# Attention scores of one transformer layer in five fp32r passes instead of two fp32 matmuls

## What is computed

```
q = (rms_norm(cq, q_norm_g) @ w_uq)      # 8 heads of 128 + 64 columns
kv = (rms_norm(ckv, kv_norm_g) @ w_ukv)  # 8 heads of 128 (keys) + 128 (values)
q_lat = concat([q_nope, axial_rope(q_rope)])
k = concat([k_nope, broadcast(axial_rope(k_rope))])   # 256 latent + 256 context tokens
s = einsum('bqhd,bkhd->bhqk', q, k) * 192 ** -0.5
out = softmax(s) @ v
```

## Time and profile before

| | us |
|---|---|
| median of three runs | 2856.29 (2855.32 to 2858.62) |
| profiled execution, its own time | 2855.02 |
| span of the profiled execution | 2853.2 |
| PE busy | 2775.5 (97% of the span) |
| DVE busy | 1699.8 (60%) |
| ACT busy | 901.1 (32%) |
| first score starts, last score starts (from the span's start) | 1941.79, 2024.4 |

### The profile page before, as it was taken

One profiled execution on the slowest core, in us unless ns is written; L12 is line 12 of the kernel. 1 busy time (PEld: TensorE's weight loads), 2 busy tenths in 40 slices (PEclk: granted clock), 3 DMA queues, 4 the chain that ended last, 5 costly groups with the idle time before them and its releaser, 6 DMA issues.

```text
span 2853.2 us, 33123 instructions
## 1 busy us (share of the span) xinstructions
PE 2775.5 (97%) x12983; PEld 2293.5 (80%) x12983; DVE 1699.8 (60%) x1740; ACT 901.1 (32%) x830; POOL 7.0 (0%) x15
## 2 busy tenths in 40 slices
PE   6999999999999999999999899999989999999998
PEld 4778888888888888878877788887878888888886
DVE  6866756666575756565645843465564555555556
ACT  6631212122121212112112522354353333333333
POOL 0000000000000000000000000000000000000000
PEclk9999999999999999999999999999999999999999
DMA  9956555555554657676755442432355555555553
GB/s 312 303 193 191 170 150 158 163 160 162 147 176 132 196 158 255 191 245 188 232 170 176 111 118 89 131 106 80 118 171 173 187 186 190 191 191 190 182 188 132
DMA packets 408016, 496.83 MB, mean 174 GB/s; under 512 B 19090, under 2 KB 277512, under 8 KB 407176
## 3 DMA queue, kind: packets, MB, share of 16 engines
q1 hardware_dynamic: 407196, 493.10, 55.3%
q0 software_dynamic: 496, 2.63, 0.3%
q10 hardware_dynamic: 252, 0.10, 0.0%
HBM read 493.69 MB, written 2.10 MB: 174 GB/s over the span
## 4 chain that ended last, share of the span: by engine, by line
PE 83%; DVE 4%; ACT 3%; issue 2%; DMA 2%; SPq 0%; DVEq 0%; ACTq 0%
PE py L944 8%; PE py L946 8%; PE py L945 8%; PE pg L944 5%; PE pg L946 5%; PE pg L945 5%; PE pu L946 5%; PE pu L945 5%; PE pu L944 5%; ACT wh L562 2%; PE py L1378 2%; PE py L1380 2%; PE py L1379 2%; PE pg L1359 1%; PE pg L1360 1%
## 5 line engine op out<-in xcount | busy, mean ns | idle before, releaser
L1450 DVE TENSOR_TENSOR wl<-raw,wh 128x2048 fp32r<-128x2048 f32 x342 | 783.7, 2291 | 832.5 <-ACT wh L562 832.3
L562 ACT ACTIVATE wh<-raw 128x2048 fp32r<-128x2048 f32 x342 | 654.1, 1914 | 1361.8 <-PE py L946 495.8
L944 PE MATMUL py<-ah,wh 128*128 128x512 f32 x704 | 276.8, 393 | 6.2 <-DVE xy L1612 5.1
L946 PE MATMUL py<-ah,wl 128*128 128x512 f32 x704 | 274.8, 390 | 0.0
L945 PE MATMUL py<-al,wh 128*128 128x512 f32 x704 | 274.6, 390 | 0.0
L944 PE MATMUL pu<-hh,wh 128*128 128x512 f32 x656 | 255.8, 390 | 0.0
L944 PE MATMUL pg<-hh,wh 128*128 128x512 f32 x656 | 255.5, 389 | 0.0
L946 PE MATMUL pu<-hh,wl 128*128 128x512 f32 x656 | 255.2, 389 | 0.0
L946 PE MATMUL pg<-hh,wl 128*128 128x512 f32 x656 | 255.2, 389 | 0.0
L945 PE MATMUL pu<-hl,wh 128*128 128x512 f32 x656 | 255.2, 389 | 0.0
L945 PE MATMUL pg<-hl,wh 128*128 128x512 f32 x656 | 255.2, 389 | 0.0
(11 more groups left out here) (420 smaller groups left out, 4605.2 us busy)
## 6 DMA issues: line engine op xcount, KB each, us to landing
raw<-in_ffn_w_in SPq DMA_DIRECT2D x170, 1024.0 KB
chunk<-in_ada_w SPq DMA_DIRECT2D x189, 512.0 KB, 3.9
raw<-in_ffn_w_out SPq DMA_DIRECT2D x88, 1024.0 KB
raw<-in_ada_w SPq DMA_DIRECT2D x64, 512.0 KB
raw<-in_mix_w_in SPq DMA_DIRECT2D x30, 1024.0 KB
accc<-in_ada_w SPq DMA_DIRECT2D x35, 512.0 KB, 4.7
raw<-in_mix_w_out SPq DMA_DIRECT2D x16, 1024.0 KB
war<-in_ffn_w_in SPq DMA_DIRECT2D x16, 384.0 KB, 5.1
```

The costliest lines, as they stand in the source:

```text
L562: nc.scalar.activation(wh[:, slot % 2, :], raw[:, slot, :], ACT.Copy).then_inc(wh_ready, 1)
L944: mm(out_ap, w[0], xh_ap, start=first, stop=False, skip_group_check=True)
L946: return mm(out_ap, w[1], xh_ap, start=False, stop=last, skip_group_check=True)
L1450: tt(wl[:, slot % 2, :], raw[:, slot, :], wh[:, slot % 2, :].bitcast(F32), ALU.subtract).then_inc(wl_ready, 1)
```

## The change

The scores are made in five fp32r passes of 512 columns each. For that, the copies `qn` and `kn` are written by ACT as fp32r (the high parts) and DVE subtracts them from the PSUM bank to get the low parts `qnl` and `knl`; it counts `upl_ready`, and PE may reuse a bank only when the low part is out too. The shared rotary key becomes `krh` (high, ACT) and `krl` (low, DVE). For the rotary queries, a tile `qs` of 128 partitions holds for each head the 64 high rows in one half and the 64 low rows in the other, so that one pass over 128 partitions against `krh` (which holds the rotary key twice) covers high x high and low x high; one pass over 64 partitions against `krl` covers high x low. `qs` is made two heads at a time by `rope_high` (two ACT copies of 64 x 256) and `rope_low` (two DVE subtractions of 64 x 256): the first pair before the attention stage, the three others inside its steps a = 0, 2 and 4. The turning of the retention output moves on PE from before the values slab to behind its sixth bank, with a wait for all four rotations, since `qs` takes the place of `yret`. ACT's `y_high` and DVE's `y_low` move with it, and so do the splits of the slab after. No load is added or moved on SP's or POOL's queue.

```diff
@@ -180,9 +180,12 @@
     cql = at("cql", [P, QT, LAT], F32R, o_e + 4 * KB)
     ckvh = at("ckvh", [P, CT, TOK], F32R, o_hl + 20 * KB)
     ckvl = at("ckvl", [P, CT, TOK], F32R, o_hl + 24 * KB)
-    qn = at("qn", [P, HEADS, LAT], F32, o_hl + 8 * KB)
+    qn = at("qn", [P, HEADS, LAT], F32R, o_hl + 8 * KB)
+    qs = at("qs", [P, HEADS, LAT], F32R, o_hh + 24 * KB)
     qr = at("qr", [P, HEADS // 2, LAT], F32, o_a)
-    kn = at("kn", [P, HEADS, TOK], F32, o_xc)
+    kn = at("kn", [P, HEADS, TOK], F32R, o_xc)
+    knl = [at("knl0", [P, 4, TOK], F32R, o_hh + 8 * KB), at("knl1", [P, 4, TOK], F32R, o_e)]
+    krl = at("krl", [P, TOK], F32R, o_e + 12 * KB)
     vm = [at("vm0", [P, 4, 4 * P], F32, o_a + 8 * KB), at("vm1", [P, 4, 4 * P], F32, o_hl)]
     pt = [at("pt0", [P, 4, LAT], F32, o_hl + 16 * KB), at("pt1", [P, 4, LAT], F32, o_e + 8 * KB)]
     pn = at("pn", [P, 2, TOK], F32, o_hl + 28 * KB)
@@ -203,6 +206,8 @@
     ropes = at("ropes", [P, 4, LAT], F32, o_m + 4 * P * 4)
     sgn = at("sgn", [P, 2, 512], F32, o_m + 4 * P * 4)
     act = sm("act", [P, TOK])
+    qnl = [at("qnl0", [P, 4, LAT], F32R, o_a + 4 * KB), at("qnl1", [P, 2, LAT], F32R, o_e + 14 * KB),
+           at("qnl2", [P, 2, LAT], F32R, small[0])]
     rms = sm("rms", [P, TOK])
     rope_t = sm("rope_t", [P, LAT])
     vt = sm("vt", [P, VROWS])
@@ -217,6 +222,7 @@
     csp = sm("csp", [P, 4 * KT + P], F32R)
     rstd = sm("rstd", [P, 12])
     ssum = at("ssum", [P, TOK], F32, small[0])
+    krh = at("krh", [P, TOK], F32R, small[0])
     rows = sm("rows", [4, 2 * BLK])
     hf = at("hf", [P, 2, TOK], F32, o_m + 4 * P * 4)
     dec = sm("dec", [P, 2 * HEADS])
@@ -291,7 +297,8 @@
     rs_done, rp_ready, ry_done, ry_free = sem("rs_done"), sem("rp_ready"), sem("ry_done"), sem("ry_free")
     yst_ready, ysd_ready, yn_ready, y_turned = sem("yst_ready"), sem("ysd_ready"), sem("yn_ready"), sem("y_turned")
     mixh_ready, mixl_ready, rg_ready, rgs_ready = sem("mixh_ready"), sem("mixl_ready"), sem("rg_ready"), sem("rgs_ready")
-    up_done, up_free = sem("up_done"), sem("up_free")
+    up_done, up_free, upl_ready = sem("up_done"), sem("up_free"), sem("upl_ready")
+    krh_ready, qsh_ready, qs_ready = sem("krh_ready"), sem("qsh_ready"), sem("qs_ready")
     sc_done, nm_ready, exp_done, pn_ready = sem("sc_done"), sem("nm_ready"), sem("exp_done"), sem("pn_ready")
     turned, pt_ready, o_done, oh_ready, ol_ready = sem("turned"), sem("pt_ready"), sem("o_done"), sem("oh_ready"), sem("ol_ready")
     sgn_ready, gu_ready, act_turned = sem("sgn_ready"), sem("gu_ready"), sem("act_turned")
@@ -312,6 +319,9 @@
     XBANKS = py + pgu
     EARLY_BANKS = ((2, pg, pu), (0, py[0], py[1]), (1, py[2], py[3]))
+
+    def qn_low(h):
+        return qnl[0][:, h, :] if h < 4 else qnl[h // 2 - 1][:, h % 2, :]
     def pair(bank_ap):
         return bank_ap.rearrange("p (a n) -> p a n", a=2)
@@ -779,6 +789,8 @@
             static_split(MIX0 + S_UQ + 1)
             se.wait_ge(decay_ready, HEADS)
             nc.scalar.activation(ckvh[:], ckv[:], ACT.Copy).then_inc(cqh_ready, 1)
+            se.wait_ge(rope_done, 9)
+            nc.scalar.activation(krh[:], krope[:], ACT.Copy).then_inc(krh_ready, 1)
             gates_out(1)
             values_out(1)
             def gates_silu():
@@ -816,11 +828,20 @@
             static_split(MIX0 + S_UQ + 4)
             for h in range(HEADS):
                 up(12 + h, kn[:, h, :], py[h % 4][:])
+            def rope_high(j):
+                se.wait_ge(rope_done, 9 + j + 1)
+                for lo in (0, ROPE):
+                    ins = nc.scalar.activation(qs[lo:lo + ROPE, 2 * j + lo // ROPE, :], qr[lo:lo + ROPE, j, :], ACT.Copy)
+                ins.then_inc(qsh_ready, 1)
+
+            se.wait_ge(yn_ready, 1)
             for k in range(4):
-                y_high(k)
-            static_split(MIX0 + S_UQ + 5)
-            se.wait_ge(mixl_ready, 4)
-            for k in range(4):
+                if k == 3:
+                    se.wait_ge(y_turned, 4)
+                    rope_high(0)
+                    for j in range(4):
+                        y_high(j)
+                    static_split(MIX0 + S_UQ + 5)
                 for half in range(2):
                     j = 20 + 2 * k + half
                     up(j, vm[half][:, k, :], py[j % 4][:])
@@ -853,6 +874,8 @@
                 probs(a)
                 if a + 2 < 16:
                     exps(a + 2)
+                if a in (0, 2, 4):
+                    rope_high(a // 2 + 1)
                 if a % 2 == 1:
                     static_split(MIX0 + S_OUTR + a // 2 + 1)
             out_high(HEADS - 1)
@@ -1228,7 +1251,11 @@
             def up_bank(k):
-                if k >= 4:
+                if 4 <= k < 12:
+                    pe.wait_ge(upl_ready, k - 3)
+                elif 16 <= k < 24:
+                    pe.wait_ge(upl_ready, k - 7)
+                elif k >= 12:
                     pe.wait_ge(up_free, k - 3)
                 return py[k % 4]
@@ -1262,9 +1289,6 @@
                     ins = three(b[:], w_at(m, t * 1024 + h * P, t * 1024 + (h + 1) * P), ckvh[:, t, :], ckvl[:, t, :],
                                 t == 0, t == CT - 1)
                 ins.then_inc(up_done if h < HEADS - 1 else slab_used, 1)
-            pe.wait_ge(yn_ready, 1)
-            for k in range(4):
-                y_turn(k)
             m = MIX0 + S_UKV + 1
             pe.wait_ge(wl_ready, m + 1)
             for k in range(4):
@@ -1277,11 +1301,14 @@
                         mm(b[:], xl_ap, w_h, start=False, stop=False)
                         ins = mm(b[:], xh_ap, w_l, start=False, stop=(t == CT - 1))
                     ins.then_inc(up_done if (k, half) != (3, 1) else slab_used, 1)
-                if k == 0:
-                    pe.wait_ge(mixl_ready, 4)
                 if k < 2:
                     for j in (2 * k, 2 * k + 1):
                         swap(9 + j, qr[:, j, :], 2)
+                if k == 2:
+                    pe.wait_ge(yn_ready, 1)
+                    pe.wait_ge(rope_done, 13)
+                    for j in range(4):
+                        y_turn(j)
             def scores(a):
@@ -1290,14 +1317,22 @@
                     pe.wait_ge(exp_done, a - 2)
                 else:
                     pe.wait_ge(up_free, 25 + a)
+                if a % 4 == 0:
+                    pe.wait_ge(qs_ready, a // 4 + 1)
                 lo = (h % 2) * ROPE
                 b = py[a % 3]
-                mm(b[:], qn[:, h, k * P:(k + 1) * P], kn[:, h, :], start=True, stop=False)
-                mm(b[:], qr[lo:lo + ROPE, h // 2, k * P:(k + 1) * P], krope[lo:lo + ROPE, :], start=False, stop=True).then_inc(sc_done, 1)
+                o = slice(k * P, (k + 1) * P)
+                mm(b[:], qn[:, h, o], kn[:, h, :], start=True, stop=False)
+                mm(b[:], qn[:, h, o], knl[h // 4][:, h % 4, :], start=False, stop=False)
+                mm(b[:], qn_low(h)[:, o], kn[:, h, :], start=False, stop=False)
+                mm(b[:], qs[:, h, o], krh[:], start=False, stop=False)
+                mm(b[:], qs[lo:lo + ROPE, h, o], krl[lo:lo + ROPE, :], start=False, stop=True).then_inc(sc_done, 1)
             def turn(a):
                 pe.wait_ge(pn_ready, a + 1)
-                if a >= 2:
+                if a < 2:
+                    pe.wait_ge(mixl_ready, a + 1)
+                else:
                     pe.wait_ge(pt_ready, a - 1)
                 for j in range(4):
                     ins = nc.tensor.transpose(pgu[a % 2][:, j * P:(j + 1) * P], pn[:, a % 2, j * P:(j + 1) * P], ident)
@@ -1319,7 +1354,6 @@
                                     mixh[:, head0 + k, :], mixl[:, head0 + k, :], k == 0 and d == 0, k == HEADS - 1)
                 ins.then_inc(slab_used, 1)
-            pe.wait_ge(rope_done, 13)
             scores(0)
             scores(1)
             for a in range(16):
@@ -1333,6 +1367,7 @@
                     pe.wait_ge(wl_ready, MIX0 + S_OUTR + h + 1)
                     if h == 0:
                         pe.wait_ge(up_free, 28)
+                        pe.wait_ge(mixl_ready, 4)
                     pe.wait_ge(y_free, Y_OUT + h)
                     out_slab(MIX0 + S_OUTR + h, py[3], 0)
                     if h < HEADS - 1:
@@ -1804,12 +1839,25 @@
             ve.wait_ge(cqh_ready, 1)
             tt(cql[:], cq[:], cqh[:].bitcast(F32), ALU.subtract).then_inc(lat_split, 1)
             static_split(MIX0 + S_UQ + 1)
+
+            def up_low(k, out_ap, in_ap, high):
+                ve.wait_ge(up_free, k + 1)
+                tt(out_ap, in_ap, high.bitcast(F32), ALU.subtract).then_inc(upl_ready, 1)
+
+            def query_lows(h0, h1):
+                for h in range(h0, h1):
+                    up_low(h, qn_low(h), py[h % 4][:, 0:LAT], qn[:, h, :])
+
             ve.wait_ge(cqh_ready, 2)
             tt(ckvl[:], ckv[:], ckvh[:].bitcast(F32), ALU.subtract).then_inc(lat_split, 1)
+            ve.wait_ge(krh_ready, 1)
```

(26 more changed lines are left out.)

## The result

The changed kernel takes 2862.14 us (median of 11 runs, 2860.36 to 2865.1) against 2855.63 us of the kernel before (11 runs): ratio 1.0021, 95% interval 1.0013 to 1.0029. It is slower by 6.5 us. Forecast were 2857.6 us and no change, so the time lies above the range.

What follows compares the result with a forecast made beforehand. PE was taken to bound the kernel; -9.2 (scores) + 2.5 (before the first score) + 2.1 (fill) + 5.9 (three steps) = +1.3 us on the profiled 2855.02, forecast 2857.6 us, no change; range 2852.5 to 2860.8.

Steps and rivals of the forecast that it cites:

- the first paragraph's rule: PE bounds the values and attention stages: a pass taken out is worth its full time, a wait costs its full time.
- The fill: Filling the softmax pipeline before turn(0): row_max(0) stands behind DVE's split, so PE stands 2.1 us.
- A rotary step: Attention steps 0, 2 and 4: row_norm stands behind rope_low, PE stands about 2.0 us each, 5.9 us together.
- part 3: Three attention steps with a rotary pair: a 3.3 us chain from turn(a) to turn(a + 1) makes PE wait, 5.9 us.
- the scores: Attention stage: each of 16 scores falls from 2.10 to 1.53 us, a gain of 9.2 us.
- The stretch ahead: Before the first score: PE waits for DVE's low parts and the values slab's split, together 2.5 us.
- The wait for the fourth rotation: Before the moved transposes on PE: costs nothing, rotations end at 1938.8, PE's sixth values bank at 1939.0.
- The new score: Five fp32r passes in 1.53 us, keeping 0.4 us for going to the 64-partition form and back.
- Rival 1: Scores: tiling switches go away with short passes, 15.6 us less on PE but longer stalls, net -2 us, 2854.4; chance 0.2.
- rival 2: Lows hide: no waits in the rotary steps, fill under 1 us; 2844 to 2850.6 us, faster; chance 0.08.
- Rival 3: Slower: the switch inside fp32r costs more, at 0.43 each +8.7 us, 2865; chance 0.06 with dearer rotary operations.
- a dearer pass: Scores: the 64-partition pass runs like its fp32 forerunner, 0.43 instead of 0.23 us, +3.2 us, the range's upper end.

Runs made afterwards that it cites:

- both orders: Changed kernel with rotary pairs made in steps 1, 3, 5 and the first output slab's split moved early: 2849.91 us, ratio 0.9973 to the kernel before.
- full-pass run: Changed kernel with the fifth pass of each score over all 128 partitions instead of 64: 2857.69 us, ratio 1.0001 to the kernel before.
- filler run: Changed kernel with ten useless fp32r passes on PE between scores(2) and turn(0): 2859.98 us, ratio 1.0014 to the kernel before.

## Why the prediction was wrong

**The part that failed** is the first paragraph's rule: "a wait put in costs its full time". A wait costs that and, in most of the profiles with waits of over 2 us, a stretch at half clock from within the wait or right behind it. The working read the clock as 1.00 in both windows of the kernel before and carried it over to a kernel with four waits of 2 us and more, although none of the rows that it rested on showed such a wait. The trace did: the 2.25 us wait at 1272 us above, with 0.50 behind it. Neither the sum nor a rival had a term for it. It is 4.0 of the 6.0 us that the attention stretch came out above the forecast; without it the profiles would differ by 3.0 us, inside the forecast range (up to 4.5 above the kernel before).

**The other 2.0 us are sizes.** The waits of fill and steps are 9.66 us instead of 8.0. The fill is 2.45 (7.05 - 4.60) instead of 2.1; row_max(0) starts 7.4 us behind the turns instead of 6.7, mostly because the two rotary copies ahead of it take longer (0.85 us instead of 0.56, begun 0.3 us after the turns). A rotary step is (9.66 - 2.45) / 3 = 2.4 instead of 2.0: the 64 x 256 copies on ACT and subtractions on DVE, which no row of the kernel before showed, take 0.41 and 0.42 us each and do not overlap, so a pair is 0.83 and 0.85 us, where the working had 0.6 and 0.7. Timelines of ACT and DVE after:

```profile
1953.37 0.83 ACT L834 ACTIVATE qs<-qr 64x256 fp32r<-64x256 f32 x2
```
```profile
1954.23 0.85 DVE L1889 TENSOR_TENSOR qs<-qr,qs 64x256 fp32r<-64x256 f32 x2 [2.44 <-ACT qs L834]
1955.12 0.16 DVE L1907 RECIPROCAL rrec<-rsum 128x1 f32<-128x1 f32 x1
```

They show the chain of part 3 as it was forecast: the reciprocal of step 1 stands behind a subtraction that waits 2.44 us for ACT. And the scores are worth 8.85 instead of 9.2 us (with both orders).

**What was right.** The stretch ahead: 2.25 us for 2.5, in the places named. Laid pass by pass beside the kernel before, the changed one loses 0.3 us at query bank 5 (forecast 0.4), 0.2 at bank 8 (0.1), 0.6 at key bank 16 (0.85) and 1.2 at the values (1.1); the view of waits lists only part of this (none, 0.3, 0.3 and 0.9). The wait for the fourth rotation cost nothing. The new score: 1.54 for 1.53 us, with the change of form kept, which the full-pass run confirms. The places of the four stalls, and the head without a rotary pair (11.37 for 11.3). With the sizes corrected and the clock added the sum is 2.25 - 8.85 + 9.66 + 4.01 = 7.07 us, and the profiles differ by 7.0; the last three terms are differences of the same four profiles, so that they add up to the 4.82 us of the attention stretch by construction.

**The rivals.** Rival 1 (no switches) and rival 2 (the lows hide) did not come. Rival 3 named the right side by a wrong mechanism: the switch cost 0.39 there and back, no more than in the earlier trace rows. Its chance of 0.06 for the slower side was far too low, since the forecast's gain and loss were both near 10 us and any cost of a stall beyond its length went to one side only. The range's upper end held a dearer pass (3.2 us) that did not come, and nothing for the stalls.

The Trainium skill, page TensorE: Matmul & The Clock Gate, section Terms, puts the penalty of the lower clock at half the time spent in it. By that rule the 13.6 us of the changed kernel's profile (1949.9 to 1960.1 and 2042.05 to 2045.5) would cost 6.8 us, by estimate; measured are 4.0. In part of that time PE stood idle: the slower score behind turn 0 lies under the wait for turn 1, which is 1.25 us here and 2.33 in the filler run. The measurement decides.

**What stays open:** why a wait of 2.3 us brings a fall in one execution and none in another, and why the second fall of the first profile (behind 1.1 + 0.7 us, a pair of waits that the kernel before has too, with the clock at 1.00) came. Nor is it shown how short a wait must be to be safe: 1.5 us brought no fall in one profile, but waits of 1.1 and 0.7 us close together brought one in two profiles. The size of the clock's part in a median rather than a profile is known only through totals: the filler run's median is 2.2 and 0.9 us below the changed kernel's two, and its profile 4.0.

## What to carry to other kernels

Where PE is the bound, a new stall of 2 to 3 us can be dearer than its length; price it with a stretch at half clock behind it (here 1.5 to 4.4 us on top, summed over the attention stretch, in five profiles with one to four waits of 2.3 to 2.8 us; nothing in the filler run's, with three of 2.3, and nothing in the one with 1.5). Look for waits of that length and the granted clock behind them in the whole trace of before, not only where the change acts. Before taking a faster form of the bounding operation, write out the in-order lists of the engines that feed it: here the faster scores were worth 8.85 us, and the waits from two misplaced items, with the clock behind them, took it all back; placed otherwise, with one pass widened to the array's full height, the same change makes the kernel 10 to 14 us faster. A pass over half the partitions among full ones costs 0.39 us for the change of form; if the other half holds valid or harmless numbers, use all of it.

## What the runs showed of the hardware that was not expected

- The granted clock fell to 0.50 within or right behind waits of PE of 2.3 to 2.8 us inside a stream that is otherwise dense, in fp32r and in fp32 matmuls alike, and stayed up behind one of 1.5 us. It fell behind some waits of 2.3 us and not behind others, and in two profiles behind waits of 1.1 and 0.7 us, which brought none in the others. In the changed kernel's first profile it was down 1.3 us into the wait.
- With ten useless matmuls in a wait the stretch behind it was 2.35 us shorter in the profile (12.93 and 10.58 us).
- One pass over 64 partitions among passes over 128 costs 0.39 us; the same pass over 128 partitions takes 0.23 us like its neighbours.
- Copies and subtractions of 64 x 256 take as long as ones of 128 x 256 (0.41 us against 0.39 on ACT, 0.42 on DVE either way) and, with one behind the other from SBUF to SBUF on ACT, start 0.42 us apart, while the 128 x 256 copies out of PSUM started 0.27 apart. No run separates the place from the partitions.
